# First block's final norm moved into the merge, both phase borders rearranged, and the fifth early z tile's split moved up its queues

## The chip, the cores and the metric
The kernel runs on one core of one Trainium2 chip. Its engines are TensorE (PE in the profile, PEld for its weight loads), VectorE (DVE), ScalarE (ACT), GpSimd (POOL) and SyncE (SP, which here only issues transfers). The metric is the device time of one execution in microseconds (us), lower is better; the kernel before takes 3202.73 us, the median of 3 runs (3202.24 to 3208.15).

## The reference
Two transformer blocks follow one another on one sequence of 1024 tokens of width 1024, all in float32. The first block ends with the MLP and a final norm; the second starts from that norm's output twice, once through its own norm and once as the residual:

```python
def first_block(x, ...):
    ...                                   # two kinds of attention, w_o, then the MLP
    h = h + jnp.einsum('bsf,fd->bsd', hid, w_down[l])
    return rmsnorm(h, final_norm_g)

def second_block(x, mem, ...):
    ...
    h = _rms_norm(x, g_pre[l])
    y = _hybrid_mixer(h, mem, w_in[l], ...)   # proj = h @ w_in + b_in, five branches, gates,
                                              # merged = sum(gate * branch_out), merged @ w_out
    x = x + _rms_norm(y, g_post[l])
```

So the value x that the second block adds at its very end is the first block's h, times one over its root mean square per token, times a gain per feature (final_norm_g).

## The kernel before
**Layout.** Features lie on the 128 partitions (DC = 8 tiles of features), tokens along the free dimension, in two halves h of 512 tokens. A product of two float32 matrices is made in three passes: each operand is split into a rounded high part and the rest, and hi*hi + hi*lo + lo*hi is summed in PSUM. For each 128x1024 tile of weights SP loads `raw`, ACT copies it to `w_hi`, POOL subtracts to make `w_lo`, and 8 feature tiles times 3 passes make 24 matmuls per half, a "unit" (about 5.5 us in the program's plan, `TICK`). Tiles go through two slots of raw, w_hi and w_lo, used in turn.

**Three phases.** `first_block`, `mixer_phase` and `merge_phase` are each a block of five instruction streams, one for each engine, under `phase(...)`. At a phase's end every engine drains, POOL clears the phase's semaphores, and a barrier of all engines follows; these rows carry lines 182, 184 and 185. Nothing of the next phase is issued before it. SP's last waits of a phase are for transfers, so that no semaphore is cleared while a transfer will still add to it.

**What sets the order.** Inside a phase each engine's stream is woven from several generators ("lanes"). Each lane yields a due time before each step, and the lane with the smallest due time is emitted next. The due time only sorts: an engine then runs its stream in order, and an instruction that waits holds up all behind it. So moving a due time moves an instruction past others in the queue, and nothing else.

**End of the first block.** `ff.units` is the list of MLP units. The 16 before the z units are the last part of w_down: 8 tiles for half 0, then 8 for half 1 (`last_down`, `d_end[h]` their planned end). DVE adds each unit's PSUM to `resid` (L1711, semaphore `joined`). `last_sums` squares it twice (ACT L1403, L1406) and adds the squares up (DVE L1838, L1842); PE turns the sums over partitions (L1097, L1100); `last_roots` makes the two roots (`root` for the final norm, `both_roots` for final and pre norm together), scales (DVE L1859) and splits the result into the second block's input (ACT L1430 `normed_hi`, DVE L1863 or POOL L1494 `normed_lo`). Then DVE multiplies `resid` itself by gain and root, 8 times per half (L1869), and SP's lane `spill` stores it in `d["res"]` (L777). Meanwhile PE does 5 units of the second block's input projection for half 0 only, the z tiles (`HALF_TILES`), whose results ACT moves out (L1368) and SP stores (L784). Three lanes split weights: for the five z tiles and for the mixer's first two tiles, which the mixer finds ready in the two slots.

**Mixer.** Its units 0 and 1 use slot 0, units 2 and 3 slot 1. Results go through three buffers `res` and are stored by ACT's queue (L2552, L2564) with `stored`; SP's lane `ends` (L2228) waits for all stores. The last two weight tiles are again for the next phase, the merge.

**Merge.** PE first does the two "plain" gate tiles (four units, L3365 to L3367), then products of gate pairs, branch units, and 16 units of w_out (L3437 to L3439): 8 tiles for half 0, 8 for half 1. During these ACT moves the result out and squares it, DVE sums squares (L3730), SP loads the residual (`residual`, L3328, one 128x512 piece each) and the w_out tiles (L3274). After each half `outputs` does `out = out * gain * root` on DVE (L3740) and `out + res` on DVE (L3744) or POOL (L3628), and SP stores it (L3340), waiting for each in turn.

## Time and profile before
| what | value |
|---|---|
| median of 3 runs | 3202.73 us |
| the profiled execution | 3199.06 us, of which its span 3197.2 us |
| busy share PE / PEld / DVE / ACT / POOL | 96 / 73 / 52 / 38 / 26 % |
| mean granted TensorE clock | 0.985 |
| first border: last matmul of block one to first of the mixer | 8.06 us of PE idle, ends at 1454.09 |
| second border: last matmul of the mixer to first of the merge | 6.32 us of PE idle, ends at 2554.51 |

The profile is one execution. The span runs from the first to the last instruction; 1.86 us of the execution's time lie outside it. Times in rows are us from the start of the span. PE is busy nearly throughout, so time is won or lost where PE stands idle, where its clock is granted at half, or after its last matmul.

### The profile page before, as it was taken

Reading aid. Unit: us, or ns where it says so; the run is one execution under the profiler, and the core shown is the slowest. Engines: PE = TensorE matmul, PEld = TensorE weight load, DVE = VectorE, ACT = ScalarE, POOL = GpSimd, SP = SyncE. Lnnn points to the kernel's source line nnn. Section 1 sums busy time; section 2 is a strip of 40 time slices with the busy share of each in tenths; the row PEclk is TensorE's granted clock in tenths of the full one; section 3 lists DMA queues with packets and bytes.
Section 4 is the critical chain, followed back from the end, with each engine's and each line's share of the span. In section 5 each row is a group of like instructions: output and inputs, shape, how many; then the busy total and the mean of one; then the engine's idle time right before and its main releaser. Section 6 shows DMA issues by size and latency. Waiting matters only on the chain. (4 is left out here: it accounts for less than half of the span.)

```text
span 3197.2 us, 39024 instructions
## 1 busy us (share of the span) xinstructions
PE 3059.8 (96%) x15417; PEld 2347.6 (73%) x15417; DVE 1656.8 (52%) x2120; ACT 1207.1 (38%) x1794; POOL 840.6 (26%) x472
## 2 busy tenths in 40 slices
PE   8999999999999999988999999999999999999997
PEld 6765544678888788867677777777777788877885
DVE  4224345556545422485366776766555242337855
ACT  4224544334333221252463333433444343443333
POOL 1222211134444222352121011102111144431234
PEclk9999999999999999999999999999999999999999
DMA  4221000033333522234432111212433223455644
GB/s 158 76 81 52 33 1 17 1 113 131 110 122 119 206 99 93 81 113 152 105 125 86 41 67 56 70 60 94 130 109 108 86 95 120 158 198 186 255 142 142
DMA packets 144877, 334.98 MB, mean 105 GB/s; under 512 B 12344, under 2 KB 53560, under 8 KB 144568
## 3 DMA queue, kind: packets, MB, share of 16 engines
q1 hardware_dynamic: 117624, 267.73, 25.1%
q10 hardware_dynamic: 27072, 64.76, 5.2%
q8 instruction: 123, 2.02, 0.3%
q14 instruction: 58, 0.48, 0.0%
HBM read 234.40 MB, written 96.99 MB: 104 GB/s over the span
## 5 line engine op out<-in xcount | busy, mean ns | idle before, releaser
L2259 PE MATMUL psum<-normed_hi,w_hi 128*128 128x512 f32 x984 | 422.6, 429 | 13.0 <-PEq L185 8.1
L2734 POOL TENSOR_TENSOR w_lo<-raw,w_hi 128x1024 fp32r<-128x1024 f32 x64 | 172.7, 2699 | 930.1 <-ACT w_hi L1912 930.1
L2261 PE MATMUL psum<-normed_hi,w_lo 128*128 128x512 f32 x984 | 387.8, 394 | 0.0
L2260 PE MATMUL psum<-normed_lo,w_hi 128*128 128x512 f32 x984 | 386.9, 393 | 0.0
L1447 POOL TENSOR_TENSOR w_lo<-raw,w_hi 128x1024 fp32r<-128x1024 f32 x80 | 201.9, 2524 | 531.3 <-ACT w_hi L1154 471.0
L2259 PEld LDWEIGHTS psum<-normed_hi,w_hi 128*128 128x128 f32 x984 | 187.3, 190 | 62.2 <-issue 23.3
L2261 PEld LDWEIGHTS psum<-normed_hi,w_lo 128*128 128x128 f32 x984 | 186.4, 189 | 41.4
L2260 PEld LDWEIGHTS psum<-normed_lo,w_hi 128*128 128x128 f32 x984 | 187.4, 190 | 37.2 <-issue 6.3
L1154 ACT ACTIVATE w_hi<-raw 128x1024 fp32r<-128x1024 f32 x80 | 84.6, 1057 | 306.4 <-PE psum L1039 260.4
L1912 ACT ACTIVATE buffer<-psum,par 128x512 f32<-128x512 f32 (+1 forms) x131 | 93.2, 713 | 258.7 <-PE psum L2261 243.9
L1711 DVE TENSOR_TENSOR res<-psum,res 128x512 f32<-128x512 f32 x80 | 55.2, 690 | 211.9 <-PE psum L1039 211.9
L1912 ACT ACTIVATE w_hi<-raw 128x1024 fp32r<-128x1024 f32 x98 | 103.6, 1057 | 161.1 <-PE psum L3439 80.0
L2783 DVE SCALAR_TENSOR_TENSOR buffer<-buffer,par,buffer 128x1024 f32<-128x1024 f32 x120 | 163.8, 1365 | 1.0
L1912 ACT ACTIVATE buffer<-psum 128x512 f32<-128x512 f32 (+3 forms) x121 | 67.5, 567 | 225.5 <-PE psum L2387 45.2
L3616 POOL TENSOR_TENSOR w_lo<-raw,w_hi 128x1024 fp32r<-128x1024 f32 x34 | 84.8, 2494 | 237.3 <-ACT w_hi L1912 236.7
L1037 PE MATMUL psum<-normed_hi,w_hi 128*128 128x512 f32 x328 | 129.8, 396 | 3.2 <-POOL w_lo L1447 3.2
L1038 PE MATMUL psum<-normed_lo,w_hi 128*128 128x512 f32 x328 | 128.1, 391 | 0.0
L1039 PE MATMUL psum<-normed_hi,w_lo 128*128 128x512 f32 x328 | 128.1, 391 | 0.0
L1189 ACT ACTIVATE buffer<-psum 128x1024 f32<-128x1024 f32 (+3 forms) x48 | 39.0, 812 | 215.6 <-PE psum L876 198.3
L3437 PE MATMUL psum<-split_parts,w_hi 128*128 128x512 f32 x288 | 113.7, 395 | 0.0
L3438 PE MATMUL psum<-split_parts,w_hi 128*128 128x512 f32 x288 | 112.1, 389 | 0.0
L3439 PE MATMUL psum<-split_parts,w_lo 128*128 128x512 f32 x288 | 112.0, 389 | 0.0
(538 smaller groups left out, 7476.5 us busy)
## 6 DMA issues: line engine op xcount, KB each, us to landing
raw<-in_w_in SPq DMA_DIRECT2D x75, 512.0 KB, 4.4
scratch_in<-buffer ACTq DMA_DIRECT2D x59, 512.0 KB, 2.6
raw<-in_w_mlp SPq DMA_DIRECT2D x42, 512.0 KB, 3.6
scratch_gate<-gate_out ACTq DMA_DIRECT2D x60, 256.0 KB, 2.0
gate_in<-scratch_gate SPq DMA_DIRECT2D x27, 512.0 KB, 4.1
scratch_hid<-hidden_out ACTq DMA_DIRECT2D x44, 256.0 KB, 4.4
split_plain<-scratch_y SPq DMA_DIRECT2D x20, 512.0 KB, 7.2
raw<-in_w_br SPq DMA_DIRECT2D x18, 512.0 KB, 5.0
```

Source lines behind the costliest of these rows:

```text
L1037: pe.matmul(bank, hi, xh, start=kk == 0, stop=False, skip_group_check=True)
L1038: pe.matmul(bank, hi, xl, start=False, stop=False, skip_group_check=True)
L1039: mm = pe.matmul(bank, lo, xh, start=False, stop=kk == DC - 1, skip_group_check=True)
L1447: pool.tensor_tensor(to[1].lo, to[0], to[1].hi.bitcast(F32), ALU.subtract).then_inc(w_lo, 1)
L1912: return self.act.activation(out, x, func, **more)
L2259: pe.matmul(out, hi, xh, start=k == 0, stop=False)
L2260: pe.matmul(out, hi, xl, start=False, stop=False)
L2261: mm = pe.matmul(out, lo, xh, start=False, stop=k == DC - 1)
L2734: pool.tensor_tensor(ws.lo[:, n % 2], raw[:, n % 2], ws.hi[:, n % 2].bitcast(F32), ALU.subtract).then_inc(w_lo, 1)
L2783: dve.scalar_tensor_tensor(acc, u[:, k:k + S], taps[:, k:k + 1], acc, ALU.mult, ALU.add).then_inc(long_chain, 1)
L3437: pe.matmul(bank, hi, xh, start=k == 0, stop=False)
L3438: pe.matmul(bank, hi, xl, start=False, stop=False)
```

## The change
1. **Final norm's output.** DVE's 16 multiplications of `resid` in the first block go. SP stores the plain `resid` as soon as it is joined, among the loads of the last w_down tiles, and the two roots in a new scratch tensor `root`. In the merge SP loads the roots (`first_root`), and a new DVE lane `first_norm` multiplies each piece of the residual by gain and root while PE does w_out. The residual loads get other due times, and from the fifth on each waits for the scaling four before it.
2. **Borders.** The waits for last stores leave the ends of `first_block` and `mixer_phase`. Their semaphores (`z_stored`, `x_stored`, `root_stored`, `tile_stored`) live in the whole program, and the next phase waits for them: SP ahead of the mixer's first loads, DVE and ACT ahead of what overwrites those buffers, SP ahead of the second gate pair. At the program's end they are cleared, with one more barrier.
3. **Second slot.** The last weight tile of each phase is only loaded there (SP waits for it to land). ACT and POOL split it as the first thing of the next phase.
4. **Last z slot.** For the fifth z tile (`len(slots) - 3`) the split's due times become `slot_due - 3.5` on ACT (was + 0.1) and `slot_due - 2.3` on POOL (was + 1.3).

```diff
@@ first_block, SP
                     for part in range(4):
-                        yield d_end[h] + 14.0 + calm[h] * (DC + 1.2 * part)
-                        sp.wait_ge(res_ready, DC * h + 2 * part + 2)
+                        n = ff.index("down", last_down + 2 * part + 1, h)
+                        yield ended(n) + 2.0
+                        sp.wait_ge(joined, ff.adds(n + 1))
                         sp.dma_start(d["res"][2 * part:2 * part + 2, :, cut]...,
-                                     resid[:, 2 * part:2 * part + 2, cut]).then_inc(spilled, 16)
+                                     resid[:, 2 * part:2 * part + 2, cut]).then_inc(m.x_stored, 16)
+                    yield d_end[h] + 9.0
+                    sp.wait_ge(fin_rooted, h + 1)
+                    sp.dma_start(d["root"][h], root).then_inc(m.root_stored, 16)
...
-                sp.wait_ge(z_out, 16 * len(HALF_TILES))
-                sp.wait_ge(spilled, 128)
+                sp.wait_ge(landed[(len(slots) - 1) % 2], 16 * ((len(slots) + 1) // 2))
@@ first_block, ACT (POOL alike, with - 2.3)
-                for n in range(len(slots)):
-                    yield step_at[T] + 4.0 if n == N_FRONT + 1 else ...
+                for n in range(len(slots) - 1):
+                    yield slot_due(n) - 3.5 if n == len(slots) - 3 else step_at[T] + 4.0 if n == N_FRONT + 1 else ...
@@ first_block, DVE
-                    for j in range(DC):
-                        yield d_end[h] + 10.2 + calm[h] * (DC + 0.6 * j)
-                        part = halves(resid[:, j])[h]
-                        dve.wait_ge(u_scaled, h * DC + j + 1)
-                        dve.scalar_tensor_tensor(part, part, m.p("final_g", j), root, ALU.mult, ALU.mult).then_inc(res_ready, 1)
@@ mixer_phase, SP
                 yield -7.0
+                sp.wait_ge(m.x_stored, 128)
+                sp.wait_ge(m.root_stored, 32)
+                sp.wait_ge(m.z_stored, 16 * len(HALF_TILES))
...
-                for r in range(3):
-                    sp.wait_ge(stored[r], 16 * ((len(held) + 2 - r) // 3))
+                sp.wait_ge(landed[(len(st.slots) - 1) % 2], 16 * ((len(st.slots) - 1) // 2))
@@ mixer_phase, ACT
+                yield -5.0
+                run(ws.hi[:, 1], raw[:, 1], ACT.Copy).then_inc(w_hi, 1)
@@ merge_phase, SP
+                    if p == 1:
+                        for r in range(3):
+                            sp.wait_ge(m.tile_stored[r], 16 * ((N_STORED + 2 - r) // 3))
...
-                        yield st.units[st.index("out", j, h)].due + 6.0
+                        yield st.units[st.index("out", 0, 0)].due + 6.0 + 4.5 * n
...
+                            sp.dma_start(first_root, d["root"].rearrange("h p t -> p h t")).then_inc(root_in, 16)
                         if n >= 4:
-                            sp.wait_ge(res_in[n % 4], 16 * (n // 4))
+                            sp.wait_ge(res_scaled, n - 3)
@@ merge_phase, ACT (POOL alike: second_lo)
+            def second_tile():
+                yield -1.0
+                run(ws.hi[:, 1], raw[:, 1], ACT.Copy).then_inc(second_hi, 1)
@@ merge_phase, DVE
+            def first_norm():
+                for h in range(2):
+                    for j in range(DC):
+                        n = h * DC + j
+                        yield st.units[st.index("out", 0, 0)].due + 12.0 + 4.5 * n
+                        if n == 0:
+                            dve.wait_ge(root_in, 16)
+                        part = halves(res[:, j])[h]
+                        dve.wait_ge(res_in[n % 4], 16 * (n // 4 + 1))
+                        dve.scalar_tensor_tensor(part, part, m.p("final_g", j), first_root[:, h], ALU.mult, ALU.mult).then_inc(res_scaled, 1)
@@ program
     first_block(nc, m, d)
     second_block(nc, m, d)
+    nc.clear_and_free_semaphores([m.z_stored, m.x_stored, m.root_stored, *m.tile_stored])
+    nc.all_engine_barrier()
```

PE's stream holds the same instructions in the same order. Three places of the others matter. First ACT at the end of block one; `normed_hi` rows make half 1 of the mixer's input, `z_half` rows move a z unit out, `w_hi` rows split a weight tile. Before:

```order
L1154 ACTIVATE w_hi_64<-raw_62 128x1024
L1368 ACTIVATE z_half_236<-psum,par_52 128x512
L1430 ACTIVATE normed_hi_58<-normed_plain_156 128x512 x5
L1154 ACTIVATE w_hi_64<-raw_62 128x1024
L1368 ACTIVATE z_half_236<-psum,par_52 128x512
L1430 ACTIVATE normed_hi_58<-normed_plain_156 128x512 x2
L1154 ACTIVATE w_hi_64<-raw_62 128x1024
L1368 ACTIVATE z_half_236<-psum,par_52 128x512
L1154 ACTIVATE w_hi_64<-raw_62 128x1024
L1368 ACTIVATE z_half_236<-psum,par_52 128x512
```

And now:

```order
L1157 ACTIVATE w_hi_64<-raw_62 128x1024
L1371 ACTIVATE z_half_236<-psum,par_52 128x512
L1433 ACTIVATE normed_hi_58<-normed_plain_156 128x512 x2
L1157 ACTIVATE w_hi_64<-raw_62 128x1024
L1433 ACTIVATE normed_hi_58<-normed_plain_156 128x512 x3
L1371 ACTIVATE z_half_236<-psum,par_52 128x512
L1433 ACTIVATE normed_hi_58<-normed_plain_156 128x512 x2
L1157 ACTIVATE w_hi_64<-raw_62 128x1024
L1371 ACTIVATE z_half_236<-psum,par_52 128x512 x2
```

The fifth z tile's w_hi passes three `normed_hi`, and the mixer's second tile's w_hi, ahead of the last z_half, is gone. Next DVE after half 0 of w_out: L3740 (now L3777) scales an output, L3744 (now L3781) adds the residual, L3730 (now L3756) sums squares, L3767 is the new scaling of a residual piece. Before:

```order
L3740 SCALAR_TENSOR_TENSOR out_21997<-out_21997,par_52,total_22001 128x512
L3744 TENSOR_TENSOR out_21997<-out_21997,res_54 128x512
L3740 SCALAR_TENSOR_TENSOR out_21997<-out_21997,par_52,total_22001 128x512 x2
L3744 TENSOR_TENSOR out_21997<-out_21997,res_54 128x512
L3740 SCALAR_TENSOR_TENSOR out_21997<-out_21997,par_52,total_22001 128x512
L3730 TENSOR_TENSOR total_22001<-squares_21999 128x512
L3740 SCALAR_TENSOR_TENSOR out_21997<-out_21997,par_52,total_22001 128x512
L3744 TENSOR_TENSOR out_21997<-out_21997,res_54 128x512
```

And now:

```order
L3777 SCALAR_TENSOR_TENSOR out_21968<-out_21968,par_52,total_21972 128x512
L3781 TENSOR_TENSOR out_21968<-out_21968,res_54 128x512
L3777 SCALAR_TENSOR_TENSOR out_21968<-out_21968,par_52,total_21972 128x512
L3767 SCALAR_TENSOR_TENSOR res_54<-res_54,par_52,first_root_21974 128x512
L3777 SCALAR_TENSOR_TENSOR out_21968<-out_21968,par_52,total_21972 128x512
L3781 TENSOR_TENSOR out_21968<-out_21968,res_54 128x512
L3777 SCALAR_TENSOR_TENSOR out_21968<-out_21968,par_52,total_21972 128x512
L3756 TENSOR_TENSOR total_21972<-squares_21970 128x512
L3767 SCALAR_TENSOR_TENSOR res_54<-res_54,par_52,first_root_21974 128x512
L3777 SCALAR_TENSOR_TENSOR out_21968<-out_21968,par_52,total_21972 128x512
L3781 TENSOR_TENSOR out_21968<-out_21968,res_54 128x512
```

Two scalings (the tenth and eleventh of 16) now stand ahead of the third DVE addition, and a twelfth ahead of the last one of that half. SP in the same stretch, now (before, the store and load pairs stand in the same way around the w_out loads):

```order
L3287 DMA raw_62<-in_w_out 128x1024
L3354 DMA out_x<-out_21968 128x512
L3342 DMA res_54<-scratch_res 128x512
L3354 DMA out_x<-out_21968 128x512
L3287 DMA raw_62<-in_w_out 128x1024
L3354 DMA out_x<-out_21968 128x512
L3342 DMA res_54<-scratch_res 128x512
L3354 DMA out_x<-out_21968 128x512 x2
L3287 DMA raw_62<-in_w_out 128x1024
```

The third w_out load here still stands behind the store of the third DVE sum (the last of the `x2`), and each store waits for its sum.

## Rows read from the trace of the kernel before

**Rows 1.** PE's waits in the whole span: us in total, times, longest.
```profile
PE psum L2259 <- PEq L185: 8.1, 1, 8.1
PE psum L3365 <- PEq L185: 6.3, 1, 6.3
PE psum L1097 <- DVE free L1838: 2.0, 1, 2.0
PE psum L3437 <- POOL w_lo L3616: 1.4, 1, 1.4
```

**Rows 2.** DVE's groups between 1394.5 and 1414 us.
```profile
L1869 DVE SCALAR_TENSOR_TENSOR res<-res,par,buffer 128x512 f32<-128x512 f32 x8 | 10.6, 1366 | 0.0
```

**Rows 3.** Timeline, 1409 to 1450 us: start, us, instruction [idle before].
```profile
1409.83 0.50 PE L1037 MATMUL psum<-normed_hi,w_hi 128*128 128x512 f32 x1 [0.28 <-POOL w_lo L1447]
1416.30 1.10 PE L1097 MATMUL psum<-free,const 128*128 128x512 f32 x2 [2.05 <-DVE free L1838]
1434.11 1.05 ACT L1154 ACTIVATE w_hi<-raw 128x1024 fp32r<-128x1024 f32 x1
1436.05 2.80 POOL L1447 TENSOR_TENSOR w_lo<-raw,w_hi 128x1024 fp32r<-128x1024 f32 x1
1438.90 0.79 PE L1037 MATMUL psum<-normed_hi,w_hi 128*128 128x512 f32 x1 [2.91 <-POOL w_lo L1447]
1440.49 2.83 POOL L1447 TENSOR_TENSOR w_lo<-raw,w_hi 128x1024 fp32r<-128x1024 f32 x1
1447.09 0.67 ACT L1368 ACTIVATE z_half<-psum,par 128x512 f32<-128x512 f32 x1
1448.28 0.84 SPq L784 DMA_DIRECT2D scratch_in<-z_half  x1
```

**Rows 4.** Stretches: us, then busy time of each engine, PE's granted clock, DMA share, GB/s.
```profile
1391.70:1394.70 3.00, 2.99 (x13) 2.50 (x14) 3.00 (x6) 1.20 (x2) 0.49 (x1) 1.00 0.54 180
1438.90:1441.70 2.80, 2.80 (x7) 2.22 (x8) 2.80 (x3) 0.00 (x0) 2.80 (x2) 0.50 0.56 177
1441.70:1446.00 4.30, 4.30 (x19) 3.26 (x17) 4.30 (x5) 0.00 (x0) 1.62 (x1) 0.97 0.30 115
```

**Rows 5.** Line 182 between 1440 and 1460 us: ns min/median/max, start.
```profile
L182 SPq COMPARE_BRANCH  x1: 37/37/37, 1452.2 to 1452.2; - x1
```

**Rows 6.** Timeline of the second border and the merge's start.
```profile
2547.80 0.39 PE L2261 MATMUL psum<-normed_hi,w_lo 128*128 128x512 f32 x1
2548.95 0.33 ACTq L2552 DMA_DIRECT2D scratch_in<-buffer  x1
2550.51 2.34 POOL L2734 TENSOR_TENSOR w_lo<-raw,w_hi 128x1024 fp32r<-128x1024 f32 x1 [8.48 <-ACT w_hi L1912]
2554.51 0.77 PE L3365 MATMUL psum<-normed_hi,w_hi 128*128 128x512 f32 x1 [6.32 <-PEq L185]
2561.92 0.69 ACT L1912 ACTIVATE gate_out<-psum,par 128x512 f32<-128x512 f32 x1 [1.91 <-PE psum L3367]
2583.72 0.69 DVE L3667 TENSOR_TENSOR partial_sums<-partial_sums,psum 128x512 f32<-128x512 f32 x1 [10.72 <-PE psum L3401]
```

**Rows 7.** Timeline of the w_out units.
```profile
3105.39 1.79 DVE L3730 TENSOR_TENSOR total<-total,squares 128x512 f32<-128x512 f32 x1 [3.65 <-ACT squares L1912]
3150.07 2.88 DVE L3744 TENSOR_TENSOR out<-out,res 128x512 f32<-128x512 f32 x1
3153.35 0.44 SPq L3274 DMA_DIRECT2D raw<-in_w_out  x1
3160.82 0.50 PE L3437 MATMUL psum<-merged_hi,w_hi 128*128 128x512 f32 x1 [1.42 <-POOL w_lo L3616]
3163.62 2.41 POOL L3616 TENSOR_TENSOR w_lo<-raw,w_hi 128x1024 fp32r<-128x1024 f32 x1 [2.85 <-ACT w_hi L1912]
```

**Rows 8.** DVE's scalings of outputs between 3138 and 3158.2 us.
```profile
L3740 DVE SCALAR_TENSOR_TENSOR out<-out,par,total 128x512 f32<-128x512 f32 x8 | 11.1, 1409 | 3.9 <-ACT total L1912 3.9
```

**Rows 9.** Line 184 between 3180 and 3200 us, in the last border.
```profile
L184 POOLq DRAIN  x1: 158/158/158, 3196.4 to 3196.4; - x1
```

More of the change, by code:

```diff
@@ L1915 @@
 Unit = namedtuple("Unit", "kind tile half slot begins")
+N_STORED = sum(j != "ab" and not 16 <= j < 24 for j in IN2_ORDER)
 class Stream:
@@ L2248, in gemm @@
                                     pe.wait_ge(ab_lo, 1)
-                                elif unit.slot >= 2:
-                                    pe.wait_ge(w_lo, unit.slot - 1)
+                                elif unit.slot >= 1:
+                                    pe.wait_ge(w_lo, unit.slot)
                             if n >= 2:
@@ L2552, in gemm @@
                                     act.dma_start(d["in2"][j], res[:, q % 3]).then_inc(stored[q % 3], 16)
-                    if unit.slot is not None and st.done_at[unit.slot] == n + 1 and unit.slot + 2 < len(st.slots):
+                    if unit.slot is not None and st.done_at[unit.slot] == n + 1 and unit.slot + 2 < len(st.slots) - 1:
                         high(unit.slot + 2)
```

65 lines of the change are left out of this document (40 added, 25 removed).

## The prediction
> **What bounds the kernel now.** I read the page's first two parts, then PE's waits over the span, then the timelines of the places that those waits name. PE is busy 96% of the span, so only its idle time, its slow clock and what follows its last matmul can be won. The waits view shows where [rows 1]: two waits for line 185, the phase borders, of 8.1 and 6.3 us; 2.0 us for the sum of squares at the end of w_down; 1.4 us in w_out for a weight tile's low part. The timeline adds, in the z units, 2.91 us for POOL's w_lo and 0.28 us ahead of the first of them [rows 3]. All of these lie where the change works. Mixer and merge between their borders keep their order, so I take them as shifted and otherwise the same.
>
> **The change, part by part.**
>
> *A. DVE without the 16 scalings.* Between 1394.5 and 1414 us eight of them take 10.6 us [rows 2], between the joins and sums of the last w_down units, though only SP's store needs them. In that stretch PE's L1097, put among the first z unit's matmuls, waits 2.05 us for the last sum of squares; behind it PE waits for nothing of this kind. Without 10.6 us of other work DVE has caught up, and the sum is made about 2 us ahead of PE. With the 0.28 us, whose tile is split by an ACT that waited for a join, A gives -2.3 us; bounds -2.3 and 0. The second half's eight run behind everything on DVE and cost nothing but the border (C).
>
> *B. The fifth z tile.* ACT makes its w_hi at 1434.11, POOL its w_lo at 1436.05 for 2.80 us, and PE, idle for 2.91 us, starts at 1438.90 [rows 3]. The slot had been free since the third z unit ended, 5.4 us before the idle time began; the w_hi stood behind five `normed_hi`, the last of which waited for DVE. Now it stands behind two. It is then made as the slot comes free, and with 1.05 + 2.8 us of splitting it is ready over 1 us ahead of PE: -2.9 us. The idle time had a second price: in the 2.8 us behind it the granted clock is 0.50 and 7 matmuls start, where 19 start in the next 4.3 us [rows 4], so 7 x (0.40 - 0.226) = -1.2 us, with the eighth -1.3. B is -4.2; bounds -4.2 and -2 (if the three `normed_hi` now held behind it make POOL late).
>
> *C. First border.* PE's last matmul ends at 1446.03, and the mixer's first starts at 1454.09. Between them ACT makes the second mixer tile's w_hi before z_half (1447.09), POOL its w_lo, SP issues the last z store at 1448.28 and waits until it has landed, leaves at 1452.2 [rows 3, 5], and 1.9 us later PE starts: drain, clearing, barrier. The store's landing and the second split go. What is late next is either ACT's z_half and SP's issue of its store, 0.1 + 0.67 + 0.4 us after PE, which with 1.9 makes a gap of 3.1 us; or POOL, whose split of the mixer's first tile ended at 1440.49 + 2.83 = 1443.3 [rows 3]. That chain (roots, DVE's scaling, `normed_hi`, POOL) starts 2.3 us sooner by A, but now has the fifth tile's split ahead of three of its steps; I place its end at 1441.6. From POOL's end to PE takes 1.66 us at the second border (2550.51 + 2.34 to 2554.51, [rows 6]). So PE restarts at 1443.3, against a last matmul that A and B put at 1439.5: a gap of 3.8 instead of 8.06, -4.2 us. Bounds: a gap of 3.1 (-5.0); POOL as late as before, restart at 1445.0 (-2.6). After 2.91 us the clock had fallen, so it falls here too, as before.
>
> A, B and C together: restart at 1443.3 instead of 1454.09, -10.7. Even with A and B at nothing the restart would follow the old last matmul by 3.1 us, at 1449.1: -5.0.
>
> *D. Second border.* Matmuls end at 2548.2; ACT issues the last store at 2548.95 for 0.33 us, POOL splits the merge's second tile until 2552.85, and 1.66 us later PE starts, after 6.32 us [rows 6]. Without that split, and without waiting for the stores, ACT's issue at 2549.3 is last: 2549.3 + 1.66 = 2550.9, a gap of 2.75. That is -3.5 us; bounds -3.1 (with SP's 1.9) and -4.8, if the clock stays up after 2.75 us: it stayed at 1.00 behind a gap of 2.60 and fell behind 2.91 [rows 3, 4].
>
> *E. The w_out units.* DVE gets 16 scalings. In half 0 one stands by each sum of squares, where DVE is idle 3.65 us in each unit [rows 7]: hidden. After half 0 there is no room. DVE makes eight output scalings, five additions and two sums without a pause, POOL three splits and three additions, and SP stores each result in turn; the w_out load at 3153.35 waits behind the store of the third DVE sum, whose addition runs 3150.07 to 3152.95, and PE waits 1.42 us for the tile at 3160.82 [rows 7]. Two new scalings ahead of that addition and a third ahead of the half's last one delay this load and the next. The price of one is not in the trace; the nearest row is the output scaling, same operation and shape, 0.75 alone, 1.41 in the mean and 2.88 at most for such work here [rows 7, 8]. At 0.75 the next but one load is 2.25 us late: its split ended at 3166.03 [rows 7], PE needed it at 3166.27, so PE loses 2.0 us in all. At the mean, 4.2 - 0.2 = 4.0. A gain is excluded, as this stretch only gets work. I take 2.3, near the lower end, since the mean of 1.41 counts POOL's work in the stretch, which does not grow.
>
> The long rows are those that meet a POOL instruction: the addition of 2.88 us started 0.06 us after POOL's split and ended 0.55 us after it. The Trainium skill (SBUF — State Buffer, "Who interferes with whom") says that a DVE instruction with two SBUF inputs and a GpSimd one that reads SBUF exclude each other, the later one blocked until the first is done. The trace agrees. By that rule the added cost is the 0.75 alone (2.0 us); by the mean of the rows it is 4.0.
>
> *F. The end.* One more clearing and barrier: the last such from 3196.4 [rows 9] to the span's end at 3197.2, +0.8 us.
>
> *At nothing.* The second tile's w_hi (1.05) and w_lo (2.4 to 2.8) at each phase's start: PE first needs them two units (10.9 us) later; in the merge ACT was idle 1.91 us ahead of its first PSUM read, and DVE, whose first sums POOL's split can hold up 2.4 us, 10.72 us later on [rows 6]. Uncovered, 1.05 us each. SP waits at the mixer's start for a z store issued 3 us earlier: at most 1 us, with loads behind it that nothing waits for within 5 us. The residual's stores now lie between w_down loads, which have a unit to spare.
>
> **Sum.** -10.7 - 3.5 + 2.3 + 0.8 = -11.1 us on the profiled execution's own 3199.06: 3188.0. The median of the runs is 3.7 us above it; less 11.1 it gives 3191.6.
>
> **Rivals.**
> 1. *DVE in w_out takes most of it back.* Each of the three scalings at 2.88: the two loads are 5.8 and 8.6 us late, PE loses 8.4 and, with a gap above 2.9 us, 1.3 for the clock. 9.7 instead of 2.3 makes -3.7: 3199.0. For it: every DVE instruction there that meets POOL is that long. Against it: POOL's instructions are as many as before, so not all three can meet a new one.
> 2. *The residual loads choke the w_out loads; slower than before.* From the fifth on each residual load waits for a scaling, and w_out loads stand behind it on SP; the scaling stands in DVE's order, behind waits for sums and for the root. If a w_out load goes out only when its tile's predecessor is done, a unit takes as long as load and split, 3153.35 to 3160.77 = 7.4 us, instead of 5.44. It decides when some 10 of the 16 units do so: 10 x 2.0 = 20 us, more than the 13.4 gained before and the 6.4 of the bound below. With all 11 from the fifth on, -13.4 + 22 = +8.6: 3211.3. Against it: four loads are under way, scalings are due 6 us after their loads, and DVE idles 3.65 us in each unit.
> 3. *The chain before the border does not move.* The sum of squares stays late because of POOL, not of the scalings (A = 0), and POOL ends at 1443.3: restart 1445.0, -9.1 instead of -10.7. 3193.2.
> 4. *The clock stays up at the second border*: -1.3, 3190.3.
>
> **How the numbers follow.** My forecast 0.55, rival 4 0.10, rival 3 0.12, rival 1 0.15, rival 2 0.08. Faster or slower by under 0.2% (6.4 us) is what a measurement of this kernel can't tell from no change; the line to faster is at 3196.3. The forecast and rivals 3 and 4 lie below it, 0.77; rival 1 is within; rival 2 is above 3209.1, save where only a few units are slowed: 0.06 and the rest within. The likeliest case alone spans 3188 (all bounds of gain, E at 2.0) to 3196 (C and B at their poor ends, E at 4.0). For 8 in 10 I go down to 3186 and up to 3199, rival 1's figure.
>
> **What would show it.** Right: no PE wait for DVE's sum of squares among the z units, nor for w_lo at the fifth; matmuls of block one ending near 1439.5 and the mixer's starting near 1443.3; at the second border a gap near 2.75 us; in w_out two waits of 2 to 3 and about 1 us for w_lo behind late loads; the last matmul to the end longer by 0.8 us. Wrong: a mixer start after 1446, a gap of 5 us or more at the second border (then something else than stores and the split held it), more than two waits in w_out, or new PE waits in the mixer or the merge's products, which I took as unchanged.

## The result

Four runs of the changed kernel have their median at 3185.11 us (3181.74 to 3189.2), four of the kernel before at 3205.44 us (3202.24 to 3210.54): ratio 0.9936, 95% interval 0.9916 to 0.9956. The forecast of 3191.6 us had the sign and the places, and the time came out 0.9 us below its range. The two profiled executions took 3199.06 and 3181.74 us, 17.3 us apart; 11.1 were forecast.

TensorE's waits in the profile after (columns as in [rows 1]; the first four rows answer to the four there):

```profile
PE psum L2262 <- PEq L185: 3.4, 1, 3.4
PE psum L3381 <- PEq L185: 2.8, 1, 2.8
PE psum L1100 <- DVE free L1841: 0.3, 1, 0.3
PE psum L3453 <- POOL w_lo L3638: 2.8, 1, 2.8
```

Both borders are short, the wait for the sum of squares is 0.3 us instead of 2.0, and the one in w_out has doubled. To place the difference I compare the start of the k-th matmul in both traces (15417 in each). A line gives by how much the difference grows over a stretch, in us:

| stretch (time in the profile after) | part | forecast | measured |
|---|---|---|---|
| 0 to 1380 | none | 0 | -4.6 |
| 1380 to 1415 | A, VectorE without scalings | -2.3 | -2.9 |
| 1428 to 1432 | B, fifth z tile | -4.2 | -4.6 |
| 1433.6 to 1443 | C, first border | -4.2 | -5.3 |
| 1456 to 2532 | none (mixer) | 0 | +2.0 |
| 2532 to 2543 | D, second border | -3.5 | -3.5 |
| 2543 to 3139 | none (merge) | 0 | -0.5 |
| 3139 to 3162 | E, w_out | +2.3 | +1.6 |
| behind the last matmul | F, the end | +0.8 | +0.5 |
| sum | | -11.1 | -17.3 |

The six parts come to -14.2, and 3.1 us more lie where the change moves nothing. Two traces cannot tell what is chance there, so the experiments had to; two more profiles of the same changed kernel stand beside this one further down.

The first border after the change (columns as in [rows 3]; the last row is the mixer's first matmul):

```profile
1433.27 2.35 POOL L1450 TENSOR_TENSOR w_lo<-raw,w_hi 128x1024 fp32r<-128x1024 f32 x1
1433.49 1.56 SPq L788 DMA_DIRECT2D scratch_in<-z_half  x2
1434.02 0.69 ACT L1371 ACTIVATE z_half<-psum,par 128x512 f32<-128x512 f32 x1 [0.56 <-PE psum L1042]
1437.41 0.55 PE L2262 MATMUL psum<-normed_hi,w_hi 128*128 128x512 f32 x1 [3.42 <-PEq L185]
```

SP leaves at 1435.1 where it left at 1452.2 [rows 5], and now GpSimd is last: its split of the mixer's first tile ends at 1435.62, and 1.79 us later TensorE starts (forecast: 1.66 behind GpSimd). Line 182 in the profile after, ns and start, bears it out: GpSimd's drain lasts until 1432.9 + 2.76 = 1435.7, the latest of all engines'.

```profile
L182 POOLq DRAIN  x1: 2762/2762/2762, 1432.9 to 1432.9; - x1
L182 ACTq DRAIN  x1: 719/719/719, 1434.0 to 1434.0; - x1
L182 SPq COMPARE_BRANCH  x1: 38/38/38, 1435.1 to 1435.1; - x1
```

At the second border ACT's store is issued at 2533.59, and TensorE starts 1.75 us behind its end, where the forecast had 1.66 (compare [rows 6]):

```profile
2533.59 0.33 ACTq L2558 DMA_DIRECT2D scratch_in<-buffer  x1
2535.67 0.47 PE L3381 MATMUL psum<-normed_hi,w_hi 128*128 128x512 f32 x1 [2.84 <-PEq L185]
```

The granted clock after the change, by stretch (columns as in [rows 4]; 0.5 is the 1.2 GHz level, 1.00 the 2.4 GHz one): up at the fifth z unit, where it had been 0.50, low behind both borders.

```profile
1428.20:1431.00 2.80, 2.80 (x14) 2.33 (x13) 2.80 (x2) 0.63 (x1) 2.52 (x2) 1.00 0.54 187
1437.40:1441.20 3.80, 3.79 (x10) 2.99 (x11) 0.24 (x5) 3.09 (x6) 2.37 (x1) 0.55 0.55 144
2535.60:2540.00 4.40, 4.33 (x12) 3.41 (x13) 4.29 (x2) 4.35 (x3) 3.21 (x1) 0.63 0.75 263
```

In w_out the load of a tile stands on SP behind an output store that waits for VectorE, is issued at 3135.18, and TensorE pays for it at 3142.71; beside it one of VectorE's new scalings takes 2.83 us, another 0.74:

```profile
3134.80 0.34 SPq L3354 DMA_DIRECT2D out_x<-out  x1
3135.18 0.43 SPq L3287 DMA_DIRECT2D raw<-in_w_out  x1
3138.32 0.74 DVE L3767 SCALAR_TENSOR_TENSOR res<-res,par,first_root 128x512 f32<-128x512 f32 x1
3140.13 2.52 POOL L3638 TENSOR_TENSOR w_lo<-raw,w_hi 128x1024 fp32r<-128x1024 f32 x1 [2.88 <-ACT w_hi L1910]
3140.37 2.83 DVE L3767 SCALAR_TENSOR_TENSOR res<-res,par,first_root 128x512 f32<-128x512 f32 x1
3142.71 0.50 PE L3453 MATMUL psum<-merged_hi,w_hi 128*128 128x512 f32 x1 [2.75 <-POOL w_lo L3638]
```

### The profile page after: what moved, and what is told of

The parts are those of the page before. It is cut to its first block and busy times, and to the rows that moved or that the text cites. A ratio compares the mean times of both kernels' runs of the same rounds, so it can differ in the third digit from the quotient of the medians.

```text
span 3179.9 us, 39040 instructions
## 1 busy us (share of the span) xinstructions
PE 3053.2 (96%) x15417; PEld 2341.2 (74%) x15417; DVE 1650.2 (52%) x2120; ACT 1207.0 (38%) x1794; POOL 841.0 (26%) x472
```

## The experiments

Fifteen kernels ran. The table gives for each the number of runs, their mean with its standard error, and the mean split in two: what the granted clock takes, (1 - mean clock) x span, summed from each run's figures, and the rest. The clock's share counts stretches in which TensorE was idle anyway, so it is somewhat too large and the rest too small; differences between kernels are what it serves for. The kernel before ran again beside each of four sets: its means there are 3204.6, 3205.0, 3204.8 and 3201.5 us (the last one beside c_after2, k_short and k_long), so the pooled rows carry a few us of difference between sets. The ratios given with each experiment compare within its own set.

| kernel | runs | mean us | clock's share | rest |
|---|---|---|---|---|
| before | 63 | 3204.3 +- 0.4 | 50.2 | 3154.1 |
| changed (with c_after, c_after2) | 14 | 3188.2 +- 1.0 | 42.8 | 3145.4 |
| u_z | 5 | 3194.3 +- 1.8 | 47.3 | 3147.1 |
| u_norm | 11 | 3197.8 +- 1.5 | 46.5 | 3151.3 |
| u_waits | 5 | 3191.9 +- 2.0 | 45.3 | 3146.6 |
| u_split | 5 | 3193.9 +- 0.8 | 45.3 | 3148.6 |
| u_both | 5 | 3192.0 +- 1.3 | 45.3 | 3146.7 |
| p_z | 11 | 3205.2 +- 1.2 | 51.3 | 3154.0 |
| p_norm | 12 | 3200.6 +- 1.3 | 48.0 | 3152.6 |
| r_before | 12 | 3202.1 +- 1.5 | 49.3 | 3152.8 |
| r_after | 6 | 3185.4 +- 1.6 | 44.0 | 3141.3 |
| w_after | 6 | 3183.4 +- 1.4 | 41.4 | 3142.0 |
| best | 5 | 3179.4 +- 1.6 | 40.0 | 3139.3 |
| k_short | 5 | 3218.0 +- 1.7 | 52.1 | 3165.9 |
| k_long | 4 | 3230.5 +- 1.6 | 62.2 | 3168.3 |

### One part undone at a time

**u_z**: the changed kernel with the fifth z tile's old due times, on ACT and likewise on GpSimd.

```diff
-                    yield slot_due(n) - 3.5 if n == len(slots) - 3 else step_at[T] + 4.0 if n == N_FRONT + 1 else ...
+                    yield step_at[T] + 4.0 if n == N_FRONT + 1 else ...
```

> The changed kernel with one part undone: the fifth z tile's split on ACT and GpSimd has its old, later due times. Theory 1 (the parts add up): TensorE waits again some 2.9 us at the fifth z unit near 1439 us, and its clock falls there once more for some 3 us (1.5 us lost), so the span is 4.6 us over the changed kernel's 3179.9, the other steps as they are; of the time before the kernel of before keeps, 12.7 us stay. Theory 2 (the stretches of low clock only move, and what one spot gains the next gives back): the stall comes back but the fall of the clock at the first border shrinks or goes in exchange, and the difference is under 3 us. The gain of 3.75 us near 1062 us, which no edit explains: if it is caused by the change, the first unit of w_down starts as in the changed kernel here and in every other variant of it; if it is chance, in one of these traces or more GpSimd's w_lo runs ahead of VectorE's last two normed_lo, as before.

Measured: ratio to the kernel before 0.9966 (0.9953 to 0.9978), mean 6.1 us above the changed kernel's. The wait is back with 2.9 us, and the clock, low for 6.8 us behind it and not for 3.4 as in the kernel before, takes 3.1 more: 6.0, less 0.4 at the border (a gap of 3.01 us, not 3.42). Theory 1's mechanism, at the size of B plus one more stretch of low clock; theory 2 is out.

**u_norm**: the 16 scalings and the residual stores behind them back in the first block, nothing of the norm in the merge.

```diff
+                    for j in range(DC):
+                        yield d_end[h] + 10.2 + calm[h] * (DC + 0.6 * j)
+                        part = halves(resid[:, j])[h]
+                        dve.wait_ge(u_scaled, h * DC + j + 1)
+                        dve.scalar_tensor_tensor(part, part, m.p("final_g", j), root, ALU.mult, ALU.mult).then_inc(res_ready, 1)
...
-            woven(sums_of_squares(), first_norm(), outputs(), ...
+            woven(sums_of_squares(), outputs(), ...
```

> The changed kernel with the final norm's 16 scalings and the residual stores behind them back in the first block, and without the root's store, the scalings and the early residual loads in the merge; both borders still without waits for last stores, and the second slot's split where the change puts it. Theory 1: TensorE waits again about 2.1 us longer for VectorE in the last stage of the first block (+3.0 before 1416 us); the border is at most 1 us longer, since no engine waits for the stores there any more and VectorE's last scaling ends before the last lower half; w_out loses its one wait of 2.8 us for GpSimd (-1.4 us), and the end is as now. Sum +1.5 to +2.6 us over the changed kernel. Theory 2 (the norm in the merge is what lets the border be short, since the stores depend on it): the mixer's first loads and VectorE's first memsets wait for the residual stores, and the border grows by 2 to 4 us, in all +4 to +6.

Measured: 0.9978 (0.9968 to 0.9988), mean +9.6 us, of which the last stage of the block has 4.5 in the trace: 2.9 of waits and 1.6 of a clock that fell. Theory 1 fell: the border is 5.8 us longer though no engine waits for a store to land. The place is SP's order. VectorE's last eight scalings run past the last matmul, the residual's stores wait for them one by one, and the last z store stands behind those. Timeline of u_norm:

```profile
1444.20 8.50 DVE L1868 SCALAR_TENSOR_TENSOR res<-res,par,buffer 128x512 f32<-128x512 f32 x8
1450.08 3.01 SPq L777 DMA_DIRECT2D scratch_res<-res  x3
1453.14 0.51 SPq L784 DMA_DIRECT2D scratch_in<-z_half  x1
1455.58 0.77 PE L2262 MATMUL psum<-normed_hi,w_hi 128*128 128x512 f32 x1 [9.16 <-PEq L185]
```

Theory 2 had the cause nearer, though the stores' issue and not their landing is what holds, and both sums were too small. In w_out the wait of 2.8 us that theory 1 had going is not gone: one of 3.38 us stands a unit later, with no scaling in the merge.

**u_waits**: SP waits at both borders for the last stores again.

```diff
+                sp.wait_ge(m.z_stored, 16 * len(HALF_TILES))
+                sp.wait_ge(m.x_stored, 128)
+                sp.wait_ge(m.root_stored, 32)
...
+                for r in range(3):
+                    sp.wait_ge(m.tile_stored[r], 16 * ((len(held) + 2 - r) // 3))
```

> The changed kernel with the waits for the last stores back at both borders: SP waits there for the z tiles', the residual's and the root's stores at the end of the first block, and for the last tiles' stores at the end of the mixer. Theory 1: the last z stores are issued at 1433.5 us and the matmuls end at 1433.6, so the barrier moves from about 1435.5 to 1436 or 1437: the first border is 1 to 3 us longer, with the clock's loss after it; at the second border ACT's last store was issued at 2533.6 and a store takes 2 to 2.5 us, so it is 1 to 2.4 us longer. Sum +2 to +5.5 us. Theory 2 (the splits of the second slot were what the borders waited for, the stores landed under them): GpSimd's last w_lo ends at 1435.6, so the first border grows by under 0.7 us, and the sum is under +2.

**u_split**: the second slot's split back in the phase before, at both borders.

```diff
-                for n in range(len(slots) - 1):
+                for n in range(len(slots)):
...
-            for n in range(1, len(st.slots) - 1):
-                pool.wait_ge(w_hi, n)
+            for n in range(2, len(st.slots)):
+                pool.wait_ge(w_hi, n - 1)
```

> The changed kernel with the second slot's split back in the phase before it, at both borders (ACT's w_hi and GpSimd's w_lo of the last slot of the first block and of the mixer), the waits for last stores still gone. Theory 1: at the first border GpSimd has one more w_lo of 2.4 us behind its last, so it ends near 1438 us instead of 1435.6 and the border is 2 to 2.5 us longer; at the second border ACT's last w_hi waits for the last matmul and GpSimd's w_lo for it, 3 to 3.5 us from the last matmul, so the border is 2 to 3.5 us longer. Sum +4 to +6. Theory 2 (the waits for the stores were the whole border): under +2.

**u_both**: both of these.

> The changed kernel with both the waits for the last stores and the second slot's split back at both borders, the final norm and the fifth z tile as the change has them. Alone, the waits made the first border 2.3 us longer and the second 3.1, the split 2.8 and 3.8. Theory 1 (both run at the same time, and the later one holds the barrier): the first border is 2.5 to 3.5 us longer than in the changed kernel, the second 3.7 to 4.2, in all 6.2 to 7.7, as with the split alone. Theory 2 (they follow one another, the stores' landing behind the split's end): 5 us and 6.9 us, in all 12.

Measured: 0.9955 (0.9941 to 0.9969), 0.9965 (0.9952 to 0.9977) and 0.9960 (0.9947 to 0.9973); the means are 3.7, 5.7 and 3.8 us above the changed kernel's, and the two borders of the traces, with the clock behind them, give 5.3, 6.6 and 6.5. The gaps of the first border are 4.7, 5.7 and 5.7 us against 3.4; of the second 5.2, 6.3 and 6.3 against 2.8. For both single ones theory 1 has the size (2 to 5.5 and 4 to 6 us). Undone together they make the gaps that the split makes alone (theory 1 of u_both): the two run side by side, and the later one holds the barrier. In u_split and u_both the second border is what it was [rows 1], 6.3 us, so taking away only the waits would have given nothing there.

### One part done alone

**p_z** is the kernel before with the fifth z tile's new due times, **p_norm** the kernel before with the norm's move alone (the changed kernel with the edits of u_z, u_waits and u_split).

> The kernel before with one part of the change alone: the fifth z tile's split on ACT and GpSimd has its new, earlier due times. Theory 1 (in the kernel before, VectorE's 16 final scalings stand between: GpSimd's earlier w_lo runs beside VectorE, both lengthen, the scalings end later against the last matmul, and SP's stores of the residual, with the last z store behind them, hold the border): the stall of 2.9 us at the fifth z unit and its fall of the clock go (-4.6 to -6.0 us), but the border's gap grows from 8.06 us to 10 to 12, and 0 to 3 us are left. Theory 2 (the parts are independent): the gap stays within 0.7 us of 8.06, and the median is 4.6 to 6 us below the kernel before's.

> The kernel before with one part of the change alone: the final norm's outputs are made in the merge from the stored residual, while the fifth z tile has its old due times, and both borders have the waits for last stores and the second slot's split. Theory 1: the last stage of the first block is 2 to 2.9 us shorter (TensorE waits 0.3 us for VectorE there, not 2.05), the stall of 2.9 us at the fifth z unit stays, the border's gap is 7 to 8 us (GpSimd's last w_lo ends 4.4 us behind the last matmul's start, and the stores land meanwhile), and w_out has one wait of 2.8 us instead of 1.4 (+1.5 us) and the end +0.6: in all 0 to 2 us faster than the kernel before. Theory 2 (the norm's move is what makes the border short): the gap is under 6 us, and it is 4 us faster or more.

Measured: p_z 1.0000 (0.9990 to 1.0010), p_norm 0.9987 (0.9976 to 0.9998). In p_z the stall at the fifth z unit is gone, and the border takes all of it back: its gap is 13.9 us instead of 8.1. The timeline of p_z shows the same queue as u_norm's, with a slower VectorE: its last eight scalings take 10.59 us, 8.53 before. That GpSimd's earlier splits are what slows it is my reading, not tested by itself.

```profile
1442.46 10.59 DVE L1869 SCALAR_TENSOR_TENSOR res<-res,par,buffer 128x512 f32<-128x512 f32 x8
1450.43 3.01 SPq L777 DMA_DIRECT2D scratch_res<-res  x3
1453.48 0.51 SPq L784 DMA_DIRECT2D scratch_in<-z_half  x1
1458.54 0.76 PE L2259 MATMUL psum<-normed_hi,w_hi 128*128 128x512 f32 x1 [13.88 <-PEq L185]
```

In p_norm the gap is 5.7 us, as in u_split and u_both, and the last stage is 2.0 us shorter. So theory 1 held for p_z, with a larger gap than its 10 to 12 us. For p_norm theory 1 had a gap of 7 to 8 us and 0 to 2 us in all, and it was theory 2's gap under 6 us that came, with a mean 3.7 +- 1.4 us below the kernel before. I had left out that the residual's stores no longer stand ahead of the last z store; the gap is 2.4 us shorter than before.

The kernel before shows the same queue, and this the forecast did not read: SP's last z store at 1448.28 us [rows 3] goes out right behind three stores of the residual, which end at 1448.23. Its copy with one wait added near 1062 us, r_before (next section), bears it out. There the clock at the fifth z unit cost 1.5 us more, and the border gave exactly that back: the gap is 6.54 us in place of 8.06. So in the kernel before, what TensorE loses or gains shortly ahead of this border is not passed on. Kernel before, then r_before:

```profile
1445.22 3.01 SPq L777 DMA_DIRECT2D scratch_res<-res  x3
1453.47 0.77 PE L2260 MATMUL psum<-normed_hi,w_hi 128*128 128x512 f32 x1 [6.54 <-PEq L185]
```

### The stretches the change does not touch

Near 1062 us the traces of before and after differ by 3.9 us with the same instructions. Before:

```profile
1060.57 4.53 DVE L1808 TENSOR_TENSOR normed_lo<-normed_plain,normed_hi 128x1024 fp32r<-128x1024 f32 x2 [3.00 <-ACT normed_hi L1361]
1061.50 5.84 POOL L1447 TENSOR_TENSOR w_lo<-raw,w_hi 128x1024 fp32r<-128x1024 f32 x2 [13.44 <-DMA scratch_hid<-relu]
```

After:

```profile
1059.84 2.36 DVE L1811 TENSOR_TENSOR normed_lo<-normed_plain,normed_hi 128x1024 fp32r<-128x1024 f32 x2 [2.80 <-ACT normed_hi L1364]
1061.10 5.70 POOL L1450 TENSOR_TENSOR w_lo<-raw,w_hi 128x1024 fp32r<-128x1024 f32 x2 [11.85 <-DMA scratch_hid<-relu]
```

If GpSimd comes first, VectorE's second instruction is held, and TensorE waits 2.3 us at once, with the clock low behind it; in the first trace it started 0.9 us behind VectorE's first, in the second 1.3 us. **c_after** and **c_after2** are the changed kernel word for word. **r_after** and **r_before** make GpSimd wait in either kernel:

```diff
                     if n == D0 + 2:
                         ...
+                        pool.wait_ge(h_lo, DC)
```

> The changed kernel word for word, once more, to see how far two executions of it differ. Theory 1: the first 1380 us, whose instructions the change leaves alone, took 4.6 us more in the kernel before's profile and 2.2 to 7.9 us more in the four variants' than in the changed kernel's, so the changed kernel's one profile was a lucky one; here those 1380 us are 2 to 8 us longer than there, in part because GpSimd's w_lo runs into VectorE's last two normed_lo near 1062 us, and the median of the runs is 3185 to 3188. Theory 2 (something in the change makes the early part faster): the early part is within 1 us of the first profile's, and the median is 3182 to 3185.

> The changed kernel with one wait more in the first block: GpSimd's w_lo of w_down's third slot waits for VectorE's eight normed_lo of the first part, so the two can't run on each other near 1062 us. Theory 1 (a race of two engines that either can win, costing 2.3 us of wait and 1.6 us of clock when GpSimd starts first): VectorE's last two normed_lo take 2.4 us together in this trace, TensorE waits 0.2 us there, and the median is 0 to 3.8 us below the unaltered changed kernel's, by how often that one loses. Theory 2 (the 3.8 us have another cause, as a late load of the hidden rows): TensorE waits over 2 us there as well, or the wait turns up at w_down's third slot, where w_lo now comes 1.1 us later.

> The kernel before with the same one wait: GpSimd's w_lo of w_down's third slot waits for VectorE's eight normed_lo. Theory 1: the stall of 2.3 us near 1062 us and the fall of the clock behind it go; against the kernel before the median is up to 3.8 us lower, ratio 0.9988 to 1.0000. Theory 2: the same as in the changed kernel's variant, no gain or a wait elsewhere.

> The changed kernel word for word a third time. Theory 1 (executions differ by where the clock is low, not by what the kernel does): the time without the clock's share is within 1.5 us of the 3145.0 us of the nine runs before, and the mean is 3185 to 3190; the first 1380 us differ by more than 1 us from both other profiles, and so do their stretches of low clock (17 and 20 us there). Theory 2: the first 1380 us repeat one of the two within 0.5 us.

Measured: c_after 0.9953 (0.9941 to 0.9965), median 3189.23; c_after2 0.9965 (0.9953 to 0.9978), median 3191.18; r_after 0.9941 (0.9930 to 0.9953); r_before 0.9991 (0.9979 to 1.0002). Of the 14 traces without the added wait GpSimd wins in 11 (TensorE then waits 2.3 us in one piece) and loses in three, the first profile of the changed kernel among them. With it TensorE's longest wait for `normed_lo` there is 0.7 to 1.1 us in all three traces (expected: 0.2). The gain of a variant is near what the runs resolve: -2.8 and -2.2 us in the means, -4.1 and -1.3 in the rest.

The first 1380 us took 5.1 and 5.5 us longer in the two copies than in the first profile, and from 2.8 us less to 7.9 us more over all traces, with low clock for 17 to 31 us in them. c_after2's rest and mean are as theory 1 had them. Its 1380 us come within 0.5 us of c_after's, which is theory 2's condition, but by delays at other places: +2.4 us near 570 us and +2.4 near 1062 in c_after2, none near 570 and +4.6 near 1062 in c_after. So I read these stretches as chance; the first profile of the changed kernel was the second quickest there of all.

The copies also show how steady the changed places are. Against the one profile of the kernel before, in us:

| part | forecast | first profile | c_after | c_after2 |
|---|---|---|---|---|
| A | -2.3 | -2.9 | -2.0 | -2.0 |
| B | -4.2 | -4.6 | -4.6 | -4.6 |
| C | -4.2 | -5.3 | -5.3 | -5.3 |
| D | -3.5 | -3.5 | -3.5 | -3.5 |
| E | +2.3 | +1.6 | +3.3 | +3.9 |
| F | +0.8 | +0.5 | +0.9 | +0.5 |
| the six parts | -11.1 | -14.2 | -11.2 | -11.0 |
| all other stretches | 0 | -3.1 | +4.5 | +4.7 |

Where the columns of E differ, TensorE's wait is the same 2.75 us, and the clock behind it is not: up in the first profile, low in both copies (c_after2 has a second wait of 0.7 us besides). The changed kernel's first profile, then c_after (columns as in [rows 4]):

```profile
3142.70:3146.10 3.40, 3.39 (x15) 2.82 (x16) 1.77 (x3) 1.21 (x2) 0.08 (x1) 1.00 0.98 292
3151.30:3154.70 3.40, 3.40 (x8) 2.72 (x9) 1.76 (x3) 0.14 (x1) 0.00 (x0) 0.50 0.91 280
```

### Two waits taken out

**w_after** places SP's output stores of the first half later in its order in w_out, **best** has this and r_after's wait.

```diff
-                        yield out_end[h] + 7.0 + (2.0 if h == 0 else 1.0) * j
+                        yield out_end[h] + (12.0 if h == 0 else 7.0) + (3.5 if h == 0 else 1.0) * j
```

> The changed kernel with SP's output stores of the first half placed later in its order in w_out (first at 12 us behind the half's end, 3.5 us apart, instead of 7 and 2), so that no load of a w_out tile stands behind a store that waits for VectorE. Theory 1 (the load issued at 3135.2 us, behind two stores that waited for VectorE, is what GpSimd's w_lo and with it TensorE's 2.8 us at 3142.7 us come from): that wait is gone or under 0.5 us, and w_out is 2.8 us shorter, or 4.4 us where the clock fell behind it (3144 to 3146 us in three of the four variants). Theory 2 (VectorE and GpSimd themselves are full there, and the load was not what they waited for): the wait stays over 2 us, or moves to a unit behind it.

> The changed kernel with both additions of the runs before: GpSimd's w_lo of w_down's third slot waits for VectorE's eight normed_lo, and SP's output stores of the first half stand later in w_out. Theory 1 (two separate stalls, each with its own gain): no wait of 2.3 us at w_down's first units and none of 2.8 us for GpSimd's w_lo in w_out, and the mean of the runs is 4 to 6 us below the changed kernel's 3187.5 (nine runs), at 3181 to 3184. Theory 2 (what these stalls cost is made good elsewhere by the clock): within 2 us of the changed kernel's mean.

Measured: w_after 0.9933 (0.9921 to 0.9945), best 0.9916 (0.9901 to 0.9930), with a median of 3180.85 us: below both kernels, and 8.8 +- 1.9 us below the changed kernel's mean, more than the 4 to 6 expected. In best TensorE waits in w_out for GpSimd no longer than this, where it was 2.8:

```profile
PE psum L3454 <- POOL w_lo L3639: 0.2, 1, 0.2
```

The late load was the cause. VectorE's new scalings and GpSimd's splits are all still there. The scalings are not needed for such a wait, though: in p_z, whose w_out is that of the kernel before, it is 4.0 us, in u_norm 3.4, and in the kernel before and r_before 1.4 and 1.2. What makes it differ with the same order was not tried.

### What a wait costs beyond its length

**k_short** adds four waits for a copy of 64 KB where TensorE has none and the clock is up, **k_long** puts two copies behind each other.

```diff
+            def stalls():
+                for i, n in enumerate(STALLS):
+                    yield st.units[n].due - 0.3
+                    sp.wait_ge(unit_done, n)
+                    sp.dma_start(d["probe"], d["root"][0, :, 0:P]).then_inc(probe, 16)
...
                         if k == 0:
+                            if n in STALLS:
+                                pe.wait_ge(probe, 16 * (STALLS.index(n) + 1))
```

> The changed kernel with four waits added in the merge's branch products (2900 to 3100 us), where TensorE is busy without a gap and its clock at full: before four of its units TensorE waits for a copy of 64 KB that SP issues when the unit before has ended (issue 0.3 us, landing 2.2 us and up, so 2.5 to 3.5 us each). Theory 1 (a wait of about 3 us can bring the clock down for 3.4 us, as behind 1439, 1601, 2536 and 3145 us, and costs its length and up to 1.7 us more): the granted clock falls behind one to four of the waits, and the stretch is 12 to 20 us longer, of them 2 to 7 by the clock. Theory 2 (the clock only falls where other things, as a phase's start, come with the wait): the clock stays at 1.00 from 2900 to 3100 us, and the stretch is longer by the waits alone, 10 to 14 us.

> The same four places, but two copies one behind the other, so 5 to 6.5 us of wait each. Theory 1: behind each of the four the clock is low for one or two stretches of 3.4 us, and each costs 1.7 to 3.4 us beyond the wait, more surely than with the short waits: the stretch is 26 to 38 us longer than the changed kernel's. Theory 2: the clock stays at 1.00, and it is 20 to 26 us.

Measured: 1.0051 (1.0037 to 1.0065) and 1.0093 (1.0079 to 1.0107). The waits came out longer than planned (the copies of k_short took 5.1 us in the median beside other loads), so the sums of both theories were too small. TensorE's waits there in k_short, then its stretch; the third fence is the changed kernel's stretch with the same 437 matmuls (us, PE busy, PEld, VectorE, ACT, GpSimd, granted clock, DMA share, GB/s):

```profile
PE psum L3464 <- DMA scratch_probe<-scratch_root: 23.1, 4, 7.3
```

```profile
2877.00:3012.00 135.00, 111.93 (x437) 87.74 (x437) 76.98 (x85) 36.84 (x35) 22.07 (x9) 0.91 0.49 177
```

```profile
2870.00:2972.00 102.00, 102.00 (x437) 81.75 (x436) 79.15 (x86) 36.43 (x35) 21.41 (x9) 1.00 0.61 227
```

33 us longer for 23.1 us of waiting: the same matmuls take 9.9 us more, 2.5 per wait. The clock fell behind all four, behind the shortest (4.00 us) for 3.4 us and behind the others for 6.8. In k_long (30.5 us of waiting, 5.16 to 9.4 each) the matmuls of the merge up to w_out start 40.8 us later, so 10.3 us are the clock's, 2.6 per wait: hardly more than for the shorter ones. Theory 1 holds for waits of 4 us and up; theory 2 is out.

For shorter waits the traces hold an experiment of their own: places where TensorE waits equally long in trace after trace. A fall of 3.4 us there costs 1.6 to 1.7 us.

| wait | place | traces with it | clock fell behind it in |
|---|---|---|---|
| 2.6 us | w_down (1387 us in the profile after) | 17 | 4 |
| 2.75 us | w_out (3142.7 us) | 11 | 9 |
| 2.78 us | merge (2825 us) | 17 | 13 |
| 2.84 us | second border of the changed kernel | 10 | 10 |
| 2.9 us | fifth z unit | 4 | 4 (twice for 3.4 us, twice for 6.8) |

## Why the prediction fell short

The places were the right ones but for a part of A, and so was what ends last at both borders. Step by step:

- **A** (forecast -2.3, its bound of gain): -2.9 between the first two profiles, in which the clock stays up here: 1.8 at the sum of squares, 0.6 at the first z unit, and 0.4 at a wait of 0.9 us for a low part, 15 us ahead of the sum, that the forecast did not have. Four traces, p_norm and both copies of the changed kernel among them, have one fall of the clock in this stretch and give -2.0 to -2.1.
- **B** (-4.2): -4.6, the wait of 2.9 us as worked out and 1.7 by the clock. But I had bounded it at -4.2 and -2 by itself; alone it is 0 (p_z), since the border then waits for VectorE and SP. B is only worth something because the norm's move takes the scalings and the stores behind them out of the way.
- **C** (-4.2): the gap went from 8.06 to 3.42 us, -4.6; I had 3.8. The last on the path is GpSimd's split of the mixer's first tile, as forecast, and it ended 1.6 us behind the last matmul where I had 2.1, so rival 3 is out. The other 0.7 is the clock: behind the border it was low for 10.2 us before and for 3.4 us after. In r_after, w_after and best, with the same gap, it was low for 6.8 us, and C is -4.1.
- **D** (-3.5): -3.5. ACT's issue is last, 1.75 us ahead of TensorE. The clock fell behind 2.84 us of waiting, so rival 4 is out. Its premise, a clock that "stayed at 1.00 behind a gap of 2.60 and fell behind 2.91", was one execution's: behind the wait of 2.6 us it fell in four traces of 17.
- **E** (+2.3): +1.6, +3.3 and +3.9 us in the three profiles. One wait of 2.75 us in place of 1.42, not two of 2 to 3 and 1 (in c_after2 a second one of 0.7), and in two of the three the clock behind it, for which the sum had no term. w_after shows the mechanism as forecast, a load behind a store that waits for VectorE. Of the scalings there one took 0.74 and one 2.83 us, so neither price of mine was the price; only which of them stood ahead of the store mattered. The rule quoted in the forecast (the Trainium skill, SBUF — State Buffer, "Who interferes with whom") agrees with this row, which starts 0.24 us behind GpSimd's split and ends 0.55 us after it, and with the two traces at 1062 us: before, the second `normed_lo` took 3.39 us and ended 1.1 us behind GpSimd's first split; after, it came first and took 1.22, and GpSimd's first split 3.35 where its second took 2.40.
- **F** (+0.8): +0.5 and, in c_after, +0.9.
- Rivals 1 and 2 (VectorE takes it back; the loads choke) did not happen: w_out has one wait for a weight tile, in c_after2 two.

**The step that failed is the clock's term of the sum.** It stood at -1.3 us, for the fifth z tile alone ("The idle time had a second price ... with the eighth -1.3"), read from one execution; the sum had none for A, C, D and E. By the means over all runs the change is worth 16.1 +- 1.1 us. The waits that went or came sum to 2.9 + 2.9 + 4.6 + 3.5 - 1.3 - 0.5 = 12.1 us; of these I had 2.3 + 2.9 + 4.2 + 3.5 - 2.3 - 0.8 = 9.8. What is left of 16.1, 4.0 us, I put down to the clock, by subtraction; the runs' own clock figures, which count idle stretches too, give 7.4 (50.2 against 42.8). So of the 5.0 us that were missing 2.3 are sizes of waits and 2.7 the clock.

Where the clock gave these back stays open. No more than 0.4 us of it was at the fifth z tile: the fall there cost 1.7 us in the kernel before, 1.9 in p_norm and 3.2 in r_before, but r_before's border handed its 1.5 back. Nor is it in the profiles: in two of the three of the changed kernel the six parts come to -11.2 and -11.0, which is the forecast. It shows in the runs' clock figures alone, not at a place.

**That the result lay outside the range has a second cause, the last line of the sum**: "3.7 us above it; less 11.1 it gives 3191.6" took three runs of one kernel as exact, and the range had no room for scatter. The differences of the means in the three comparisons of the same two kernels are 20.6, 15.8 and 12.0 us, so some 4 us of the first are which executions were caught. The changed kernel's medians in the three are 3185.11, 3189.23 and 3191.18, the mean of its 14 runs is 3188.2: all but the first lie in the range. The steadiest figure of the study is the rest without the clock's share, 3144.7, 3145.2 and 3146.1 in the three sets, 8.7 us below that of the kernel before.

Not settled: why the clock falls at one place in one execution and not in the next, with the same instructions and waits (at 2825 us: +1.6 in 13 traces, 0 in the first profile of the changed kernel, in r_before, best and k_short).

## What to carry to other kernels

A wait of the busy engine can be worth more than its length: here 2.5 us more for each wait of 4 us and up, and 0 to 3.2 for one of 2.6 to 2.9 us, differing from execution to execution. So price a removed wait with the clock, read that price from several executions, and give the forecast's range room for their scatter. Before a stall upstream of a border is removed, ask what ends last at the border: if it is another engine's queue, the gain is handed over to it whole (p_z, and the 1.5 us of r_before), and only the pair of edits pays. On an in-order DMA queue look at what each issue waits for: moving a store behind a load was worth 4.8 +- 1.7 us in the mean here, with no instruction removed.

## What the hardware showed that I had not expected

- The first 1380 us, with the same instructions but for one added wait, take up to 10.7 us more in one profiled execution than in another; the clock is low there for 17 to 31 us, and one race, decided by a lead of 0.9 or 1.3 us, adds 2.3 us of wait.
- The clock's loss hardly grows with the wait: 2.5 us for waits of 4.0 to 7.3 us, 2.6 for 5.2 to 9.4.
- The clock fell behind the wait of 2.84 us at the second border in all ten traces that have it, and behind one of 2.6 us in four of 17.
